# Second block's ffns: one half-wide plain tile, then 21 tiles by seven products of unnormalised x; ScalarE weights two chunks of x; silu one copy earlier

## The reference, cut to what matters

```
h = rmsnorm(x, ffn_norm_w[l])                       # x * rsqrt(mean(x*x) + eps) * w
u = causal_dwconv(h @ ffn_w_up[l], conv_w, conv_b)  # 1024 -> 2 * 2752, three taps over tokens
gate, val = jnp.split(u, 2, axis=-1)
x = x + (silu(gate) * val) @ ffn_w_down[l]          # 2752 -> 1024
```

## Time and profile before

| what | value |
|---|---|
| median of 3 runs | 2165.68 us (2165.32 to 2166.57) |
| profiled execution: time / span of its instructions | 2165.68 us / 2163.6 us |
| TensorE busy | 2153.1 us, 100% of the span |
| VectorE / ScalarE / GpSimd busy | 1507.8 / 597.0 / 459.0 us |
| granted TensorE clock | 0.999 of full speed |

### The profile page before, as it was taken

How to read it: one execution, slowest core, us unless ns; L and a number is a source line. 1 busy time by engine, 2 the same in 40 slices (tenths; PEclk the granted TensorE clock), 3 DMA queues, 4 the chain that set the end, 5 groups by cost and what they waited for, 6 DMA issues and landing times.

```text
span 2163.6 us, 44071 instructions
## 1 busy us (share of the span) xinstructions
PE 2153.1 (100%) x17524; PEld 2071.0 (96%) x17524; DVE 1507.8 (70%) x3184; ACT 597.0 (28%) x1608; POOL 459.0 (21%) x652
## 2 busy tenths in 40 slices
PE   9999999999999999999999999999999999999998
PEld 8999999899999999999998999999989999889998
DVE  6774856787776677668477777665758774768775
ACT  2210233512221022004433222201425520434530
POOL 1110003600222022100153002211214431313440
PEclk9999999999999999999999999999999999999999
DMA  9556654443664566456544545555636646637653
GB/s 256 164 163 181 165 141 127 137 144 118 188 168 156 169 171 171 162 166 166 148 118 124 169 132 163 164 178 143 181 99 174 174 156 168 175 98 180 163 164 109
DMA packets 571605, 340.40 MB, mean 157 GB/s; under 512 B 45332, under 2 KB 567432, under 8 KB 571400
## 3 DMA queue, kind: packets, MB, share of 16 engines
q1 hardware_dynamic: 566736, 335.46, 55.0%
q10 hardware_dynamic: 4392, 1.08, 0.2%
q0 software_dynamic: 272, 1.05, 0.1%
HBM read 336.49 MB, written 1.05 MB: 156 GB/s over the span
## 4 chain that ended last, share of the span: by engine, by line
PE 85%; issue 8%; POOLq 3%; POOL 2%; DVE 1%; DVEq 0%; ACT 0%; ACTq 0%
PE bank L1105 40%; PE bank L1183 15%; PE bank L719 8%; PE bank L788 4%; PE bank L728 3%; PE bank L905 3%; PE bank L1381 2%; PE bank L1348 1%; PE bank L1341 1%; PE bank L1055 1%; POOLq L2308 1%; POOL arena L2310 1%; PE bank L1230 1%; PE bank L1530 1%; POOLq L2326 1%
## 5 line engine op out<-in xcount | busy, mean ns | idle before, releaser
L1105 PE MATMUL bank<-work,arena 128*128 128x128 f32 x3096 | 387.9, 275 | 0.0
L1105 PEld LDWEIGHTS bank<-work,arena 128*128 128x128 f32 x3096 | 366.4, 192 | 0.0
L2403 DVE TENSOR_TENSOR arena<-ring 128x512 f32<-128x512 f32 (+1 forms) x424 | 282.3, 706 | 93.0 <-PE bank L1183 77.7
L1183 PE MATMUL bank<-gates,arena 128*128 128x128 f32 x1584 | 216.1, 275 | 0.0
L1183 PEld LDWEIGHTS bank<-gates,arena 128*128 128x128 f32 x1584 | 196.2, 192 | 0.0
L1105 PE MATMUL bank<-hT,ring 128*128 128x128 f32 x1392 | 183.9, 275 | 0.0
L1105 PEld LDWEIGHTS bank<-hT,ring 128*128 128x128 f32 x1392 | 169.6, 192 | 0.5 <-DVE work L2403 0.2
L1105 PE MATMUL bank<-work,ring 128*128 128x128 f32 x1264 | 166.3, 275 | 0.0
L2169 POOL TENSOR_TENSOR small<-small 128x2 f32<-128x2 f32 x17 | 13.4, 789 | 707.4 <-DVE small L2400 685.1
L2403 DVE TENSOR_TENSOR arena<-arena,ring 128x512 f32<-128x512 f32 (+1 forms) x212 | 146.8, 692 | 19.6
L1737 ACT ACTIVATE hT<-xT 128x512 f32<-128x512 f32 x48 | 30.1, 629 | 466.2 <-DVE xT L2406 440.4
(11 more groups left out here) (485 smaller groups left out, 3973.0 us busy)
## 6 DMA issues: line engine op xcount, KB each, us to landing
ring<-in_ffn_w_gu SPq DMA_DIRECT2D x174, 512.0 KB, 5.2
ring<-in_w_in SPq DMA_DIRECT2D x126, 512.0 KB, 5.1
ring<-in_ffn_w_down SPq DMA_DIRECT2D x112, 512.0 KB, 4.5
ring<-in_ffn_w_up SPq DMA_DIRECT2D x84, 512.0 KB, 5.3
ring<-in_w_out SPq DMA_DIRECT2D x16, 1024.0 KB, 5.1
ring<-in_ca_w_kv SPq DMA_DIRECT2D x8, 1024.0 KB, 5.2
ring<-in_ffn_w_down SPq DMA_DIRECT2D x24, 256.0 KB, 2.9
ring<-in_w_in SPq DMA_DIRECT2D x20, 256.0 KB, 4.1
```

The source lines that it names most:

```text
L1105: mm = pe.matmul(out_, a[:, c, :], b_[:, c, :], start=(start and c == 0), stop=(c == 3), skip_group_check=True)
L1183: mm = pe.matmul(bank[4 * half + where_][:, S * part + P * m:S * part + P * (m + 1)], stat[name][:, k, P * m:P * (m + 1)], moving, start=( ...
L2403: return v.tensor_tensor(out_, a, b, op)
```

## The change

- **Second block, order.** ORDER2 becomes (21, 0, 1, ..., 20), EARLY2 = 1 and LOADS2 = (1, 0, 2, ...). Only the half-wide tile 21 is plain; tiles 0 to 20 are seven products, of xg instead of hT. `turn_h` and hT go away here; the boundary is called with `turn=True`. One `make_sums` moves ahead of the boundary.
- **Second block, scaling.** Since the products are unnormalised, VectorE multiplies a4 by rbc (128x256, after a drain) before `gate_ready`, and GpSimd multiplies b4 by rbc after its addition; for this it waits for the fifth copy (`snapped` + 5) and `gate_ready`.
- **Second block, waits.** TensorE waits for the weight sums one half at a time (before the second and before the third product); `norm_step(0)` stands before the third product of the first such tile, `norm_step(1)` before its fifth.
- **First block.** With early = 0, silu(f-1) is done before the third copy (k == 2) of tile f. For f = 0 the up part and guT are made between the two halves of `make_sums`.
- **Before the first ffn of layer 1**, ScalarE multiplies chunks 6 and 7 by the norm weight (two ACT.Copy with scale, ahead of its squares of these chunks), VectorE only chunks 2 and 3 of that half.

```diff
-        ORDER2 = (0, 1, 21) + tuple(range(2, 21))
-        EARLY2 = 3
-        LOADS2 = (0, 1, 3, 2) + tuple(range(4, 22))
+        ORDER2 = (21,) + tuple(range(21))
+        EARLY2 = 1
+        LOADS2 = (1, 0) + tuple(range(2, 22))
...
@@ TensorE, ffn2_s
-                    b11, b12, b21, b22 = hT[:, 0:4, 0:P], hT[:, 0:4, P:S], hT[:, 4:8, 0:P], hT[:, 4:8, P:S]
+                    b11, b12, b21, b22 = xg[:, 0:4, 0:P], xg[:, 0:4, P:S], xg[:, 4:8, 0:P], xg[:, 4:8, P:S]
-                    pe.wait_ge(sem["sums_made"], 2 * i + 2)
+                    def ahead(k):
+                        if k in (1, 2):
+                            pe.wait_ge(sem["sums_made"], 2 * i + k)
+                        if q == 0 and k == 1:
+                            pe.wait_ge(sem["t_ready"], turned)
+                        if q == 0 and k == 2:
+                            norm_step(0.5 if late[0] else 0)
+                        if q == 0 and k == 4:
+                            norm_step(1)
+                            factors_in[0] = 5
...
@@ ScalarE, norm
+                    if k == 3 and gained:
+                        act.activation(xg[:, 6, :], xT[:, 6, :], ACT.Copy, scale=gained(6))
+                        act.activation(xg[:, 7, :], xT[:, 7, :], ACT.Copy, scale=gained(7)).then_inc(sem["xg_ready"], 1)
@@ ScalarE, first block ffn_s
-                        if k == 3 and f:
+                        if f and k == (3 if early else 2):
                             silu(f - 1)
...
@@ GpSimd, ffn2_s
-                    pool.tensor_tensor(b4[:, p % 4, P:S], keep[:, 3, :], keep[:, 1, :], ALU.add)\
+                    pool.tensor_tensor(b4[:, p % 4, P:S], keep[:, 3, :], keep[:, 1, :], ALU.add)
+                    pool.drain()
+                    pool.wait_ge(sem["snapped"], snap0 + 5 * q + 5)
+                    pool.wait_ge(sem["gate_ready"], gate0 + p + 1)
+                    pool.tensor_tensor(b4[:, p % 4, :], b4[:, p % 4, :], rbc[:, :], ALU.mult)\
                         .then_inc(sem["up_summed"], 1)
...
@@ VectorE, first block ffn_s
+                    if f == early_ == 0:
+                        make_sums(up_part)
+                    else:
+                        make_sums()
+                        up_part()
@@ VectorE, boundary_s
-                    for c in (4 + 2 * p, 2 * p):
+                    for c in (2 * p,) if turn and p else (4 + 2 * p, 2 * p):
@@ VectorE, ffn2_s
-                row_factors(make_sums)
+                row_means()
+                make_sums()
+                v.wait_ge(sem["rstd_spread"], n("rstd_spread"))
+                v.tensor_copy(rbc[:, :], bank[1][:, 0:S])
+                v.drain()
                 raw(0)
-                turn_h()
-                raw(1)
-                conv(0)
-                raw(2)
-                conv(1)
-                make_sums()
-                product(0)
-                conv(2)
...
-                    tt(a4[:, j, 0:P], keep[:, 0, :], rb, ALU.add).then_inc(sem["gate_ready"], 1)
-                    if p < len(ORDER2) - 1:
+                    tt(a4[:, j, 0:P], keep[:, 0, :], rb, ALU.add)
+                    v.drain()
+                    tt(a4[:, j, :], a4[:, j, :], rbc[:, :], ALU.mult).then_inc(sem["gate_ready"], 1)
+                    if p == EARLY2:
+                        make_sums()
+                        conv(0)
+                    elif p < len(ORDER2) - 1:
                         product(p - 2)
                         make_sums()
...
@@ VectorE, second block
-                boundary("add", lambda c: gain2(l, 8, c))
+                make_sums()
+                boundary("add", lambda c: gain2(l, 8, c), turn=True)
```

More of the change, by code:

```diff
@@ L1110, in ffn2_s @@
                 gu0, gate0, snap0 = n.value("gu_ready"), n.value("gate_ready"), n.value("snapped")
[L1111 to L1122, removed]
+                i = len(sum_slots) % 3
+                sums_in[0] = [sums[(k - i) % 3] for k in range(3)]
+                banks.first((2, 3))
+                slots.next(2)
+                first_slot = (slots.r, slots.loaded)
+                view, loaded = slots.next(2)
+                pe.wait_ge(*loaded)
+                b = free("up_done")
+                up(b, view.rearrange("p (c n) -> p c n", n=S), 0, P, xg, first=True).then_inc(sem["up_done"], 1)
+                turned = n("t_ready", 3)
+                factors_in[0] = 1
                 for q in range(len(ORDER2) - EARLY2):
@@ L1730, in load, with norm @@
                 act.dma_start(dst, src).then_inc(sem[name], 16)
-            def norm(order=range(4), two=False):
+            def norm(order=range(4), two=False, gained=None):
                 for k in order:
                     act.wait_ge(sem["x_ready"], n("x_ready"))
+                    if k == 3 and gained:
+                        act.activation(xg[:, 6, :], xT[:, 6, :], ACT.Copy, scale=gained(6))
+                        act.activation(xg[:, 7, :], xT[:, 7, :], ACT.Copy, scale=gained(7)).then_inc(sem["xg_ready"], 1)
                     ins = act.activation(hT[:, 2 * k:2 * k + 2, :], xT[:, 2 * k:2 * k + 2, :], ACT.Square)
@@ L1947, in silu @@
                     act.activation(a4[P - w:P, p % 4, :], e4[0:w, p % 4, :], ACT.Silu).then_inc(sem["silu_done"], 1)
[L1949 to L1957, removed]
+                n("up_done")
+                seen("act", "up_done")
                 for p in range(EARLY2, len(ORDER2) + 1):
@@ L1969, in ffn2_s @@
                     snap(0, 1, ra)
-                    gate_tap(p - 1)
+                    if q:
+                        gate_tap(p - 1)
                     snap(1, 2, rc)
-                    if q == 0:
-                        silu(p - 2)
-                    else:
+                    if q:
                         act.wait_ge(sem["up_summed"], n("up_summed"))
@@ L1981, in ffn2_s @@
                     snap(3, 5, ra)
-                    silu(p - 1)
+                    if q == 0:
+                        gate_tap(0)
+                    if q == 1:
+                        silu(0)
+                    if q:
+                        silu(p - 1)
                     if p < len(ORDER2):
@@ L2112, in _ @@
                 ffn_s()
-                norm((2, 0, 3, 1), two=(l == DEPTH - 1))
+                norm((2, 0, 3, 1), two=(l == DEPTH - 1),
+                     gained=(lambda c: gain("ffn1", l + 1, c)) if l + 1 < DEPTH else None)
             for l in range(DEPTH):
@@ L2801, in product @@
                     tt(guT[P - w:P, f, :], a4[P - w:P, p % 4, :], up_, ALU.mult).then_inc(sem["gu_ready"], 1)
-                row_factors(make_sums)
-                raw(0)
-                turn_h()
-                raw(1)
-                conv(0)
-                raw(2)
-                conv(1)
-                make_sums()
-                product(0)
-                conv(2)
+                row_means()
+                make_sums()
+                v.wait_ge(sem["rstd_spread"], n("rstd_spread"))
+                v.tensor_copy(rbc[:, :], bank[1][:, 0:S])
+                v.drain()
+                raw(0)
                 for p in range(EARLY2, len(ORDER2)):
```

45 lines of the change are left out of this document (22 added, 23 removed).

## The result

The changed kernel takes 2173.75 us (median of 5 runs, 2173.52 to 2173.83), the kernel before 2166.32 beside it (5 runs, 2165.32 to 2166.8): a ratio of 1.0035, 95% interval 1.0024 to 1.0046. It is 7.4 us slower, where 2.8 less was predicted.

What follows compares the result with a forecast made beforehand. TensorE was taken to bound the kernel, busy for 2153.1 of 2163.6 us. The terms -2.9 + 0.6 - 0.8 + 0.9 - 0.6 gave -2.8 us, from 2165.68 to 2162.9 us; range 2160.5 to 2166.3.

Steps and rivals of the forecast that it cites:

- Part 1: Second block, two full tiles per layer from plain to seven products: 135.47 us instead of 136.92, 1.45 less per layer.
- The cover of the start: Start of the second block's ffn: three chains in time with margins of 0.35 to 0.5 us, so no wait priced.
- Part 2, the steady part: Second block's tile loop: multiplications by rbc add 0.84 us to VectorE's 9.66 of 12.50 per two tiles, costing nothing.
- fourth rival: VectorE becomes the bound in the second block, from 2.0 us of hold-up per pair: 2173.8 us; chance 0.07.
- Part 2, the tail: After the second block's last tile: wait before the second down pass of 0.3 us per layer, bounds 0 and 0.6.
- Part 3 (a): First block, silu a copy earlier: wait before the second pass shrinks by 0.28 us in three ffns, 0.8 in all.
- Part 3 (b): First block's second ffns: table load ahead of the third copy makes TensorE wait 0.66 us, net 0.46 each, 0.9 together.
- Part 4: Before layer 1's first ffn: ScalarE takes two chunks, so TensorE waits 0.5 us less; bounds 0.3 and 1.0.
- The sum: All terms together: -2.9 + 0.6 - 0.8 + 0.9 - 0.6 = -2.8 us, so 2162.9 us.
- The range: Whole kernel time from 2160.5 to 2166.3 us, leaving out the case of VectorE as the second block's bound.

Runs made afterwards that it cites:

- silu late: Changed kernel with ScalarE's silu of a tile put behind the second copy of the next tile in the second block's ffns: 2172.71 us, ratio 1.0031.
- VectorE's alone: Changed kernel with GpSimd's multiplication of the up rows by rbc left out in the second block, VectorE's kept: 2165.37 us, ratio 0.9996.
- turned sums short: Changed kernel with GpSimd's turned sums in the second block's tile loop cut to one operation of two elements: 2165.39 us, ratio 0.9999.

## Why the prediction was wrong, by its own steps

- **Part 1 (two tiles to seven products)** was right. Predicted 135.47 us, measured 135.44 and 135.43 wherever VectorE kept up. The cover of the start held in all its three chains: the second tile begins at 1622.90, before the 1623.13 that I had worked out.
- **Part 2, the steady part, failed**: "So nothing in the steady part". It cost 139.76 - 135.44 = 4.32 us in layer 0 and 4.36 in layer 1, 8.7 in all. Two errors made it. I priced VectorE's addition at 0.84 a pair, and the stretching that comes with both multiplications, 1.86, at nothing; VectorE's multiplication alone already brought 1.51. And I held busy time against the window, 9.66 + 0.84 of 12.50, as if all of the rest could be used; 0.63 of it lies between instructions. The point from which the fourth rival decides is thus 12.51 - 0.63 - 10.50 = 1.4 us of hold-up per pair, not 2.0, and 1.86 was there. The times of the chain behind it were off too: GpSimd's product was to be ready 1.8 us into the next tile and ScalarE to want it at 2.3. It was ready at 2.6 (1663.71, the tile starts at 1661.08), since GpSimd's multiplication waits for a late VectorE, and ScalarE waited 0.16.
- **The fourth rival** had 0.07 and named mechanism and time (2173.8). That the time fits to 0.1 us is luck. It had 2.52 us of hold-up per pair and no gaps, measured were 1.86 and 0.63, which is nearly the same sum; it took the loss over all pairs, 10.9 us, where 8.7 came in the tiles and 1.3 more than forecast in the tail. I gave it little because VectorE lost 0.4 where one pair of operations met. But the steady loop has a dozen GpSimd operations per pair, and nearly all of them meet VectorE once it is late.
- **Part 2, the tail**: predicted 0.3 per layer, measured 0.93. The bound of 0.6 didn't hold it. The cause was the one named, VectorE's multiplication ahead of the sums; the size was wrong. I let GpSimd's multiplication take the turned sums' place, but the sums meet it and then three turned sums, and last 3.56 us from first start to last end, not 3.3. VectorE was also late from the tiles: its multiplication starts 0.11 after TensorE's first pass, where the sums had started 0.5 ahead of it.
- **Part 3 (a)** was right: the waits before the second pass are 0.13 instead of 0.40, three times.
- **Part 3 (b)** was right: TensorE waits 0.64 and 0.64 where 0.66 was predicted, 0.43 and 0.44 net. The first silu starts 1.29 after the load does, so a drain after the load doesn't show here either:

```profile
547.50 0.28 ACT L1931 ACTIVATE topw<-bank 128x128 f32<-128x128 f32 x1 [0.83 <-PE bank L1105]
547.80 1.28 ACT L1915 ACT_TABLE_LOAD   x1
549.09 0.42 ACT L1915 ACTIVATE e<-a 128x256 f32<-128x256 f32 x1
```

- **Part 4** was right: TensorE's wait fell from 0.85 to 0.32, and the ffn behind it runs 0.54 us earlier.
- **The sum**: -3.0 + 8.7 + 1.9 - 0.8 + 0.9 - 0.7 is 7.0, and 0.35 comes from an attention wait of layer 1 (L912, 0.96 instead of 0.61): 7.35 of 7.4. This last wait is there in every kernel with the waits in the tail (the changed one, silu late, VectorE's alone, turned sums short) and also in the one whose tail was mended by putting the sums first; in all others it is 0.6. Its cause stays open. The two profiled executions differ by 7.9 us in their spans; the other 0.5 lies in front of the first plain instruction of the program (16.68 against 16.17), ahead of everything that was changed; that stretch varies from 15.86 to 16.68 over the kernels here.
- **The range**: its upper end, 2166.3, is 0.3 too high by its own terms (2162.9 + 2.0 + 0.6 + 0.5 = 2166.0).

## What to carry to other kernels

Before work is added to an engine "with room", count its gaps between instructions as used, and add what the neighbour on the same ports costs: here the multiplication of the up rows on GpSimd (0.73 to 1.30 us) cost VectorE 0.6 to 0.7 us a tile, and 0.5 where VectorE did it itself. Two additions that each fit (11.17 and 11.04 of 12.51) can overflow together. And a bound of this kind shows in no list of waits; take the period of the loop and look for the engine that has no wait in it.

## What was not expected of the hardware

- Two GpSimd multiplications of 128x256 (0.73 to 1.30 us each) added 1.4 us on average to VectorE's unchanged instructions in a pair of tiles (1.1 to 1.75); four of them, two in a row each time (0.93 to 1.17 each), no more than 1.56. A single 128x512 sum of VectorE went from 0.69 to 1.06 beside GpSimd, the two operations of a convolution from 1.04 to 1.79.
- VectorE full with 12.36 us busy of 12.99: some 0.03 us on average is lost between two of its instructions, and no view calls it a wait. In three kernels the busy time and these 0.63 us make up the pair: 12.36 of 12.99, 12.18 of 12.81, 11.87 of 12.50.
